# Float32 weights split in pairs of tiles: one rounding and one subtraction over 1024 columns, with the remainder written over the raw weights

## What is computed

```python
def reference(x, norm_gain, w_in, attn_sinks, lb_logits, hgrn_norm_gain,
              w_up_attn, w_up_hgrn, w_out, final_norm_gain):
    B, S, _ = x.shape
    lower_bounds = jnp.cumsum(jax.nn.softmax(lb_logits.astype(jnp.float32), axis=0), axis=0)
    for l in range(DEPTH):
        h = rmsnorm(x, norm_gain[l])
        proj = jnp.einsum('bsd,dn->bsn', h, w_in[l])
        qa, ka, va, za, qb, fb, ib, zb, ga, gb = jnp.split(proj, SPLIT_POINTS, axis=-1)
        a = window_sink_attention(qa, ka, va, attn_sinks[l]) * jax.nn.silu(za)
        ob = hgrn2_chunkwise(qb, fb, ib, lower_bounds[l])
        ob = ob * lax.rsqrt(jnp.mean(ob * ob, axis=-1, keepdims=True) + EPS)
        ob = ob.reshape(B, S, HGRN_V_WIDTH) * hgrn_norm_gain[l].astype(jnp.float32)
        b = ob.astype(x.dtype) * jax.nn.silu(zb)
        y = (jax.nn.sigmoid(ga) * jnp.einsum('bsc,cd->bsd', a, w_up_attn[l])
             + jax.nn.sigmoid(gb) * jnp.einsum('bsc,cd->bsd', b, w_up_hgrn[l]))
        x = x + jnp.einsum('bsd,de->bse', y, w_out[l])
    return rmsnorm(x, final_norm_gain)
```

## Time and profile before

| | |
|---|---|
| time, median of 3 runs | 2718.64 us (2716.52 to 2720.26) |
| the profiled execution's own time | 2718.89 us |
| its span, first to last instruction | 2717.1 us |
| PE busy | 2672.5 us, 98% of the span |
| DVE busy | 1614.5 us, 59% |
| ACT busy | 1447.8 us, 53% |
| DMA queue q1, share of the 16 engines' time | 61.7% |
| granted TensorE clock, mean | 0.998 |

### The profile page before, as it was taken

The page is one execution under the profiler, slowest core; times in us unless marked ns, Lnnn a source line. Parts: engine busy times, 40 slices in busy tenths (PEclk is TensorE's granted clock), DMA queues, the critical chain, the costliest instruction groups (busy, mean ns, idle before and its releaser), DMA issues.

```text
span 2717.1 us, 39928 instructions
## 1 busy us (share of the span) xinstructions
PE 2672.5 (98%) x12249; PEld 2219.6 (82%) x12249; DVE 1614.5 (59%) x3055; ACT 1447.8 (53%) x2373; POOL 0.2 (0%) x4
## 2 busy tenths in 40 slices
PE   7999999999999999999999999999999999999997
PEld 5888888888878888888888888888888888888886
DVE  6557777777777775555555555555555555655554
ACT  5546556566555565555554444444444444554544
POOL 0000000000000000000000000000000000000000
PEclk9999999999999999999999999999999999999999
DMA  6666555565555565656666666666666666666665
GB/s 207 191 189 176 163 169 172 161 174 174 157 175 164 164 178 172 182 171 178 174 192 193 193 188 193 191 191 193 192 191 190 193 189 194 201 217 205 214 212 184
DMA packets 258546, 503.06 MB, mean 185 GB/s; under 512 B 15568, under 2 KB 15776, under 8 KB 258080
## 3 DMA queue, kind: packets, MB, share of 16 engines
q1 hardware_dynamic: 258464, 502.05, 61.7%
HBM read 497.80 MB, written 4.19 MB: 185 GB/s over the span
## 4 chain that ended last, share of the span: by engine, by line
PE 95%; DVE 2%; issue 1%; ACT 1%; DMA 0%; SPq 0%; ACTq 0%; DVEq 0%
PE acc L393 30%; PE acc L395 30%; PE acc L394 30%; PE lev L413 1%; DVE w_lo L842 1%; DVE lev_m L913 1%; PE acc L405 1%; DVE at_m L920 1%; PE lev L415 0%; DMA sink<-in_attn_sinks_dram 0%; PE lev L543 0%; ACT sq_x L674 0%; PE mis L441 0%; PE mis L426 0%; PE lev L450 0%
## 5 line engine op out<-in xcount | busy, mean ns | idle before, releaser
L842 DVE TENSOR_TENSOR w_lo<-raw,w_hi 128x512 fp32r<-128x512 f32 x1856 | 1262.2, 689 | 917.5 <-ACT w_hi L592 917.1
L592 ACT ACTIVATE w_hi<-raw 128x512 fp32r<-128x512 f32 x1856 | 1148.6, 629 | 1040.0 <-PE acc L395 1033.1
L393 PE MATMUL acc<-w_hi,h_hi 128*128 128x512 f32 x3200 | 1267.2, 396 | 7.2 <-DVE w_lo L842 6.6
L394 PE MATMUL acc<-w_hi,h_lo 128*128 128x512 f32 x3200 | 1246.7, 390 | 2.1 <-issue 2.1
L395 PE MATMUL acc<-w_lo,h_hi 128*128 128x512 f32 x3200 | 1248.0, 390 | 0.0
L393 PEld LDWEIGHTS acc<-w_hi,h_hi 128*128 128x128 f32 x3200 | 601.5, 188 | 136.1 <-DVE w_lo L842 14.8
L395 PEld LDWEIGHTS acc<-w_lo,h_hi 128*128 128x128 f32 x3200 | 601.0, 188 | 129.6 <-issue 2.3
L394 PEld LDWEIGHTS acc<-w_hi,h_lo 128*128 128x128 f32 x3200 | 601.7, 188 | 120.7
L393 PE MATMUL acc<-w_hi,a_hi 128*128 128x512 f32 x256 | 99.6, 389 | 0.0
L394 PE MATMUL acc<-w_hi,a_lo 128*128 128x512 f32 x256 | 99.6, 389 | 0.0
L395 PE MATMUL acc<-w_lo,a_hi 128*128 128x512 f32 x256 | 99.6, 389 | 0.0
(11 more groups left out here) (162 smaller groups left out, 1066.0 us busy)
## 6 DMA issues: line engine op xcount, KB each, us to landing
raw<-in_w_in_dram SPq DMA_DIRECT2D x672, 512.0 KB, 3.6
raw<-in_w_out_dram SPq DMA_DIRECT2D x128, 512.0 KB, 3.7
raw<-in_w_up_attn_dram SPq DMA_DIRECT2D x64, 512.0 KB, 3.6
raw<-in_w_up_hgrn_dram SPq DMA_DIRECT2D x64, 512.0 KB, 3.6
xr<-in_x_dram SPq DMA_DIRECT2D x8, 512.0 KB, 4.5
x_in<-in_x_dram SPq DMA_DIRECT2D x3, 1024.0 KB, 8.1
out_dram<-xr SPq DMA_DIRECT2D x6, 512.0 KB, 4.8
fgain<-in_final_norm_gain_dram SPq DMA_DIRECT2D x8, 256.0 KB, 5.9
```

Source lines behind the costliest of these rows:

```text
L393: nc.tensor.matmul(o, l_hi[:, kt, tok], w_hi[:, s, :], start=kt == 0, stop=False)
L394: nc.tensor.matmul(o, l_lo[:, kt, tok], w_hi[:, s, :], start=False, stop=False)
L592: nc.scalar.activation(w_hi[:, k % RING, :], raw[:, (k // 2) % RING, k % 2, :], ACT.Copy).then_inc(hi_ready, 1)
L842: nc.vector.tensor_tensor(w_lo[:, k % RING, :], raw[:, (k // 2) % RING, k % 2, :], w_hi[:, k % RING, :].bitcast(F32), ALU.subtract).then_i ...
```

## The change

`w_hi` grows to four pairs. `w_lo` gets no memory of its own: it lies over `raw`, of the same size, and DVE writes the remainder onto the place of the raw weights that it reads. So memory stays as it was (`raw` 4 pairs, `w_hi` 2 + `w_lo` 2 pairs before; `raw`/`w_lo` 4 pairs, `w_hi` 4 pairs now). ACT and DVE work on both tiles of a pair with one instruction of 1024 columns, at even k; at odd k they do only the side work. PE waits once for a pair. `hi_ready` and `lo_ready` count pairs. And SP may reload a pair only when PE is done with it (`pe_done`), as its memory now holds `w_lo`. `step_t`, which nothing calls, is removed.

```diff
-        raw = sb("raw", [P, RING, 2, BLK])
-        w_hi = sb("w_hi", [P, RING, BLK], F32R)
-        w_lo = sb("w_lo", [P, RING, BLK], F32R)
+        w_hi = sb("w_hi", [P, RING, 2, BLK], F32R)
+        raw_base = nc.sbuf_base
+        sb("raw_region", [P, RING * 2 * BLK])
...
+        raw, _ = at(raw_base, "raw", [P, RING, 2, BLK])
+        w_lo, _ = at(raw_base, "w_lo", [P, RING, 2, BLK], F32R)
...
-                        sp.wait_ge(lo_ready, c * (2 * RING) + n(2 * r - 2 * RING + 2))
+                        sp.wait_ge(pe_done, c * (2 * RING) + n(2 * r - 2 * RING + 2))
...
-                s = k % RING
+                s, half = (k // 2) % RING, k % 2
                 if kt == 0 and free is not None:
                     pe.wait_ge(*free)
-                pe.wait_ge(lo_ready, n(k + 1))
+                if half == 0:
+                    pe.wait_ge(lo_ready, n(k + 2, 2))
...
                 if k % 2 == 0:
                     act.wait_ge(w_landed[(k // 2) % RING], (n(k, 2 * RING) + 1) * 16)
-                if not (fresh and k < RING):
-                    act.wait_ge(pe_done, n(k - RING + 1))
-                nc.scalar.activation(w_hi[:, k % RING, :], raw[:, (k // 2) % RING, k % 2, :], ACT.Copy).then_inc(hi_ready, 1)
+                    if not (fresh and k < 2 * RING):
+                        act.wait_ge(pe_done, n(k - 2 * RING + 2))
+                    nc.scalar.activation(w_hi[:, (k // 2) % RING, :, :], raw[:, (k // 2) % RING, :, :], ACT.Copy).then_inc(hi_ready, 1)
...
-                dve.wait_ge(hi_ready, n(k + 1))
-                nc.vector.tensor_tensor(w_lo[:, k % RING, :], raw[:, (k // 2) % RING, k % 2, :],
-                                        w_hi[:, k % RING, :].bitcast(F32), ALU.subtract).then_inc(lo_ready, 1)
+                if k % 2 == 0:
+                    dve.wait_ge(hi_ready, n(k + 2, 2))
+                    pair = (k // 2) % RING
+                    nc.vector.tensor_tensor(w_lo[:, pair, :, :], raw[:, pair, :, :], w_hi[:, pair, :, :].bitcast(F32), ALU.subtract
+                                            ).then_inc(lo_ready, 1)
```

More of the change, by code:

```diff
@@ L320, in load_first @@
                     for r in range(RING):
-                        sp.wait_ge(lo_ready, c * (2 * RING) + (2 * r - 2 * RING + 2))
+                        sp.wait_ge(pe_done, c * (2 * RING) + (2 * r - 2 * RING + 2))
                         sp.dma_start(raw[:, r, :, :], w[:, bass.ds(c * (2 * RING) + 2 * r, 2), bass.ds(col, BLK)]
@@ L368, in _, with step_r @@
         def _(pe):
-            def step_t(n, k, par, r_hi, r_lo, kt, last, free):
-                s = k % RING
+            def step_r(n, k, par, l_hi, l_lo, kt, last, free, rows_done=None):
+                s, half = (k // 2) % RING, k % 2
                 if kt == 0 and free is not None:
                     pe.wait_ge(*free)
-                pe.wait_ge(lo_ready, n(k + 1))
[L375 to L389, removed]
+                if half == 0:
+                    pe.wait_ge(lo_ready, n(k + 2, 2))
                 for t in range(TT):
@@ L392, in step_r @@
                     tok = slice(t * P, (t + 1) * P)
-                    nc.tensor.matmul(o, l_hi[:, kt, tok], w_hi[:, s, :], start=kt == 0, stop=False)
-                    nc.tensor.matmul(o, l_lo[:, kt, tok], w_hi[:, s, :], start=False, stop=False)
-                    m = nc.tensor.matmul(o, l_hi[:, kt, tok], w_lo[:, s, :], start=False, stop=last)
+                    nc.tensor.matmul(o, l_hi[:, kt, tok], w_hi[:, s, half, :], start=kt == 0, stop=False)
+                    nc.tensor.matmul(o, l_lo[:, kt, tok], w_hi[:, s, half, :], start=False, stop=False)
+                    m = nc.tensor.matmul(o, l_hi[:, kt, tok], w_lo[:, s, half, :], start=False, stop=last)
                     if last and t == 0 and rows_done is not None:
```

## The result

| | before | after |
|---|---|---|
| time, median of 4 runs each, side by side | 2718.23 us | 2736.12 us (2734.55 to 2736.84) |
| the profiled execution's own time | 2718.89 us | 2736.42 us |
| its span | 2717.1 us | 2734.4 us |
| granted TensorE clock, mean | 0.998 | 0.998 |

The ratio is 1.0064, with a 95% interval of 1.0049 to 1.0079. The forecast was 2739 us, the range 2724 to 2754.

A forecast was written before the change was run, and what follows sets the result against it. PE, busy for 98% of the span, was taken as the bound. Terms 12.8 + 0.8 + 0 + 5.6 + 0.45 + 0.3 = 20.0 us on 2718.89 gave 2738.9, forecast 2739 us, range 2724 to 2754.

The forecast's parts named there:

- The saved instructions: Fewer, wider roundings and subtractions: ACT saves 199 us and DVE 143 us, both costed at nothing because these engines are idle longer.
- Attention, tile 6: Step 6 of each attention head: the pair's longer chain makes PE wait, 0.8 us per head, 16 heads, 12.8 us lost.
- L = 0.90: Lateness in us of PE's weight load at step 6 of an attention head, whose load was to start at 1063.94.
- L - 0.1: Rule for PE's lost time when a weight load starts late by L; bounds L - 0.23 and L.
- HGRN, tiles 18 and 22: HGRN heads: the pair behind the sum ends 0.04 us later, 20 x 0.04 = 0.8 us lost, bounds -2 and +3.
- The 20 stalls: PE's weight load waits for `w_lo` in HGRN before the change, 14.8 us together, 0.7 us each; forecast to stay.
- HGRN, tile 8: HGRN heads: a pair takes 0.96 us more, 0.2 us stays to spare, so 0 lost; upper bound 3 us.
- HGRN too: Rival: smaller prefetch bites also in HGRN, 16 heads by 0.3 to 1.2 us on top, 2744 to 2758 us; chance 0.15.
- Merge: Merge stage: no change, as 1.5 us to spare in place of 2.3 still covers the worst landing, 4.9 us.
- Output projection: Output block starts: first weight pair lands late behind slices of x and gain, 5.6 us lost, bounds 0 and 10.
- Tile 4 of the first output block: Output block 0: tile 4 is already late and the pair takes 0.54 us longer, 0.45 us lost.
- Start: Kernel's first step: it needs a pair, 2.29 us in place of 1.92 for two single tiles, 0.3 us lost.

## Why the prediction was right, point by point

**The saved instructions: nothing.** Right. The saving was counted at 143 and 199 us; by the busy times of the two groups it was 130 on DVE and 168 on ACT, since two narrow instructions in a row overlap a little and the wide rounding took 1059 ns in the mean, not 1044. No stage got faster by it.

**Attention, tile 6: 12.8 us, measured 12.7.** The mechanism was right link by link. In the kernel after, the maximum starts later behind the wide subtraction; ACT's exponentials and its rounding of the pair follow, and the weight load waits for DVE. The same head, ACT, then PE's weight load:

```profile
1061.16 0.40 ACT L634 ACTIVATE s_sb<-s_sb,negm 128x128 f32<-128x128 f32 x1 [2.95 <-DVE negm L944]
...
1062.18 1.04 ACT L580 ACTIVATE w_hi<-raw 128x1024 fp32r<-128x1024 f32 x1
```

```profile
1064.54 0.19 PEld L381 LDWEIGHTS acc<-w_hi,h_hi 128*128 128x128 f32 x1 [0.94 <-DVE w_lo L832]
```

In the earlier trace rows the rounding starts 1.03 us after the exponentials, here 1.02. The chain from there: 1.04, then DVE at 1063.26 for 1.23, end 1064.49, load 0.05 later. The wait of 0.94 is a little more than the L = 0.90 that was worked out; the head as a whole lost 0.81 to 0.86 in the twelve heads beside attention inputs and 0.69 to 0.71 in the four of the first merge block. The rule "L - 0.1" held, but for these four.

**HGRN, tiles 18 and 22: 0.8 us, measured 1.2 for all that the 16 heads lost.** The 20 stalls stayed, as forecast. DVE from k = 20 on, in the kernel after:

```profile
288.45 0.23 DVE L903 TENSOR_TENSOR lev_m<-mis,tab 128x64 f32<-128x64 f32 x1 [2.32 <-PE lev L403]
...
289.38 0.28 DVE L904 TENSOR_TENSOR lev_m<-lev,tab 128x128 f32<-128x128 f32 x1
289.69 2.02 DVE L910 TENSOR_REDUCE at_m<-lev_m 128x128 f32<-128x1024 f32 x1
291.63 2.35 DVE L832 TENSOR_TENSOR w_lo<-raw,w_hi 128x1024 fp32r<-128x1024 f32 x2
```

The sum starts 0.31 us behind the mask's last piece, as the prediction's "0.28 + a wake" has it, and the pair stands behind it. Each of the first twelve heads lost 0.04 to 0.18 us. The prediction had these stalls as fixed. They weren't: the subtractions in another place take 12 to 13 us away, in either kernel.

**HGRN, tile 8: 0, measured 0, but closer than said.** The prediction had 0.2 us to spare; the trace has 0.05 to 0.09 in eleven of the 16 heads, which is hardly more than a wake, and up to 0.27 in the others. (The head at step 128 loses 0.2 at its step 8, the next two 0.05.) In the four experiments with wide pairs, whose loads land sooner, it is 0.05 to 0.47. The kernel with two narrow instructions adds a little at just this place and loses in 12 of 16 heads. The rival "HGRN too" was thus nearer than its 0.15 says: only a few tenths of a microsecond per pair would have brought it.

**Merge: 0, measured 0.00.** The spare time of the steady state is 1.51 us (forecast 1.5), SP issues 0.23 us after its release (estimated 0.25). The landings of the merge stage scatter less than in the earlier trace rows:

```profile
DMA to landing us min/median/max: 3.2/3.6/4.0
```

4.0 in place of 4.9. The late reload is enough for this: the kernel with that change alone has 3.7 at most in merge, and all seven kernels with the late reload have 3.7 to 4.0, where the three with the early one have 4.6 to 4.9. The loads of before started in bursts, these start evenly spaced; that this is why is my reading, not tested.

**Output projection: 5.6 us without tile 4, measured 5.8.** The mechanism is right, as the run with the slices spread shows, but the size is right partly by luck: the parts are off and cancel. Block 1 was forecast to have no delay and has the largest, 1.7 us; its first load took

```profile
DMA to landing us min/median/max: 6.9/6.9/6.9
```

where before it had taken 4.5, and block 2's took 5.7 where the earlier trace rows had 7.2. So the long landing of the table was not bound to block 2. Block 2 lost 0.6 where 2.0 was forecast, and the five blocks after it 0.6 to 1.0 each, 4.0 in all where 3.0 was forecast. The slice in the middle of block 0, forecast at 0.6, cost nothing, with 0.1 us to spare. That is 6.4 us at the block starts, of which 0.6 came back within the blocks. (The profile books the wait of block 1 as "issue", so it is not among the 44.) In the run with the pair moved in attention, where the output stage has the same code, block 1 lost 0.9 and block 2 lost 2.0. To read the block starts as one group with one long landing somewhere was right; to give block numbers to a scatter of a single execution was not.

**Tile 4 of the first output block: +0.45 forecast, -0.2 measured.** This step failed. It took the late tile of the earlier trace rows and added the pair's longer subtraction. The pair came out a little earlier against PE than the tile had: the work ahead of it on DVE, `add_b` among it, also ran earlier. The prediction had held that work fixed. Why it ran earlier is argued only: DVE has fewer instructions there.

**Start: +0.3 forecast, -0.5 measured.** The first step of after starts at 23.27 us, of before at 23.48. The first block scatters by more than this between single executions of the same code, so neither number is borne out or refuted.

**What was not forecast.** Two places. At step 128, the first HGRN head, ACT loads a table ahead of the rounding, and here the pair came late (ACT, then PE's weight load, kernel after):

```profile
204.02 1.28 ACT L580 ACT_TABLE_LOAD   x1 [1.86 <-DMA raw<-in_w_in_dram]
205.31 1.06 ACT L580 ACTIVATE w_hi<-raw 128x1024 fp32r<-128x1024 f32 x1
```

```profile
207.68 0.19 PEld L381 LDWEIGHTS acc<-w_hi,h_hi 128*128 128x128 f32 x1 [0.61 <-DVE w_lo L832]
```

The landing that ACT waited for:

```profile
DMA to landing us min/median/max: 4.3/4.3/4.3
```

The table load alone did not cost the 0.6 us. The four experiments with wide pairs have it at the same place, their load landed after 3.3 to 3.5 us there, and PE lost nothing. It took both, 1.28 us on ACT and a landing 0.9 us longer than theirs, to use up what a pair has to spare. And at step 512 the kernel before had a wait that the kernel after doesn't have, 2.3 us, told below. Against the forecast, start and step 512 together gave 3.1 us back and tile 4 another 0.6, step 128 took 0.6, and this is why the time came out at 2736 and not at 2739. Of the two large terms attention has hardly an error, and the output projection none in its sum.

**On the pages.** In the kernel after the wide subtraction has a mean of 1224 ns. The Trainium skill, VectorE: DVE Perf Modes, section on the TRN2 errata, has a formula for fp32 that gives 1224 ns for 1024 columns, an estimate from that page; the trace agrees to the nanosecond, and the time doesn't follow. The Trainium skill, Perfetto Trace Analysis, section Optimizing Scalar/DVE Operations, says that where an engine is not saturated and another waits for it, smaller instructions may let work finish sooner. The runs agree only in part. To group single tiles by order and waits alone cost 17.5 us, so grouping does hurt here. But smaller instructions inside a pair, with one signal for both, cost 8.7 us more and saved nothing, and with the pair moved in attention 12.6 us came back with the size unchanged. What hurt was what the grouped work stands ahead of and what waits for all of it.

## What to carry to other kernels

With PE busy for 98%, fewer and larger instructions on the engines beside it were worth nothing by their sum. Ask at each place where side work stands between two weight tiles how long the chain to the next tile gets, and compare this with the time to spare there. When such a place stalls, move the weight work ahead of the wait of the side work before changing its size: two such moves, together with the slices loaded apart, were worth 32 us here, and narrower instructions at the same places cost 9. And of a stall that is already there ask the same, since the 20 old ones were worth 12 us in the unchanged kernel by one move. The side work then stands behind the landing of the tile that was moved, so look at what is to spare there too.

## What the runs showed of the hardware

**A wait of PE for nothing at the end of a loop.** In the kernel before, PE stood still once in step 512, the first behind the exit of the HGRN loop. The stop lies between the second and the third weight load of the step, where the kernel has no wait; the profile gives no releaser for it ("issue"). The waits of the kernel before, and the weight load:

```profile
PEld acc L395 <- issue: 2.3, 1, 2.3
PE acc L394 <- issue: 2.1, 1, 2.1
```

```profile
807.82 0.19 PEld L395 LDWEIGHTS acc<-w_lo,h_hi 128*128 128x128 f32 x1 [2.27 <-issue]
```

The step took 3.6 us in place of 1.36. In all four kernels with single tiles it is longer (3.6, 2.8, 3.7 and 2.3 us), in all six with pairs it is 1.36. The kernels with pairs have half as many waits of PE and a PE program that is 176 instructions shorter. That the wait is a fetch of instructions at the exit of the loop, and that the shorter program avoids it, fits this, but no run tests it.

**What is ahead in the queue.** In the kernel after a weight load of 512 KB lands in 3.2 to 4.0 us in merge, and in 5.3 to 6.9 us when 768 KB of slices were issued just ahead of it. With the slices spread over the block the first load of a block lands in 3.2 to 3.5 us again (4.1 in block 1). The load right behind the slice of x, 512 KB, then takes 4.2 to 5.0 us, and no load of that stage takes longer.
